# Attention, spectra, convolution, merge and experts in one block of a diffusion-transformer layer, with the first filter set computed in attention's tail

## The reference

```python
hx = _rms(x, norm1) * (1 + sc1) + sh1
zx = hx @ w_in
y_a = _hyena(zx[..., :OFF_Q], conv_w, conv_b, _hyena_filters(L, *filt), hyena_bias)
q, k, v = ...                                   # 8 heads, 2 key/value heads, rotary
y_b = _window_attention(q, k, v, kc, vc, attn_sink)
x_new = x + g1 * _merge(y_a, y_b, zx[..., OFF_G:], w_branch_a, w_branch_b, w_out)
hx2 = _rms(x_new, norm2) * (1 + sc2) + sh2
x_new = x_new + g2 * _expert_choice(hx2, router, w_gate, w_up, w_down)

# in _hyena_filters: four sets (2 orders x 2 halves of the channels) in the kernel
h = (h @ fout).reshape(L, HYENA_ORDER, 2, HYENA_W) * decay
k = jnp.concatenate([h[:, :, 0], zeros, h[:0:-1, :, 1]], axis=0)
return jnp.fft.rfft(k, axis=0)                  # the spectra

# in _expert_choice
aff = jax.nn.softmax(h @ router, axis=-1)
g, idx = lax.top_k(jnp.swapaxes(aff, 1, 2), cap)    # cap = 128 tokens for each expert
```

## Time and profile before

| | us |
|---|---|
| median of 3 runs (lowest, highest) | 2165.69 (2163.97, 2168.26) |
| the profiled execution, its own time | 2169.22 |
| span of its trace | 2167.4 |
| busy in the span: PE, DVE, ACT, POOL | 2125.7, 1683.4, 1174.8, 192.9 |
| DMA moved, mean rate | 540.62 MB, 249 GB/s |

### The profile page before, as it was taken

One profiled execution on the slowest core, in us unless ns is written; L12 is line 12 of the kernel. 1 busy time (PEld: TensorE's weight loads), 2 busy tenths in 40 slices (PEclk: granted clock), 3 DMA queues, 4 the chain that ended last, 5 costly groups with the idle time before them and its releaser, 6 DMA issues.

```text
span 2167.4 us, 28107 instructions
## 1 busy us (share of the span) xinstructions
PE 2125.7 (98%) x10395; PEld 1705.1 (79%) x10395; DVE 1683.4 (78%) x1820; ACT 1174.8 (54%) x1274; POOL 192.9 (9%) x85
## 2 busy tenths in 40 slices
PE   9999999989989999999999999999999999999998
PEld 4988888766669777788678888888888888888886
DVE  4667765258775999854889889898898998989986
ACT  4421222156521222334267777777777787777775
POOL 1000000000000000300001111010110111011100
PEclk9999999999999999999899999999999999999999
DMA  8234354130012234543599999999999999999993
GB/s 316 66 104 159 132 189 151 47 127 15 16 49 78 78 117 183 164 163 117 216 409 401 401 400 380 402 382 378 379 386 400 382 378 378 390 398 378 380 377 112
DMA packets 183003, 540.62 MB, mean 249 GB/s; under 512 B 14597, under 2 KB 56935, under 8 KB 182288
## 3 DMA queue, kind: packets, MB, share of 16 engines
q1 hardware_dynamic: 172872, 507.85, 62.1%
q0 software_dynamic: 5264, 17.00, 3.0%
q10 hardware_dynamic: 4792, 14.74, 1.7%
HBM read 503.90 MB, written 35.65 MB: 249 GB/s over the span
## 4 chain that ended last, share of the span: by engine, by line
PE 51%; POOL 0%; issue 0%; DVE 0%; POOLq 0%
PE p_y L312 5%; PE p_y L314 5%; PE p_y L313 5%; PE p_b L312 5%; PE p_b L314 5%; PE p_b L313 5%; PE p_a L314 5%; PE p_a L312 5%; PE p_a L313 5%; PE p_t L2875 1%; PE p_a L2905 1%; PE p_t L2866 1%; PE p_b L2905 1%; PE p_y L2961 0%; POOL out_x L2678 0%
## 5 line engine op out<-in xcount | busy, mean ns | idle before, releaser
L2745 DVE TENSOR_TENSOR r_lo<-ring,r_hi 128x2048 fp32r<-128x2048 f32 x372 | 838.8, 2286 | 59.3 <-ACT r_hi L2706 58.1
L2706 ACT ACTIVATE r_hi<-ring 128x2048 fp32r<-128x2048 f32 x372 | 708.5, 1916 | 148.9 <-PE p_b L314 76.7
L312 PE MATMUL p_y<-r_hi,a_hi 128*128 128x512 f32 x512 | 205.3, 401 | 0.0
L314 PE MATMUL p_y<-r_hi,a_lo 128*128 128x512 f32 x512 | 199.9, 391 | 0.0
L313 PE MATMUL p_y<-r_lo,a_hi 128*128 128x512 f32 x512 | 199.2, 389 | 0.0
L312 PE MATMUL p_b<-r_hi,x_hi 128*128 128x512 f32 x496 | 193.1, 389 | 0.0
L314 PE MATMUL p_b<-r_hi,x_lo 128*128 128x512 f32 x496 | 193.0, 389 | 0.0
L313 PE MATMUL p_b<-r_lo,x_hi 128*128 128x512 f32 x496 | 192.9, 389 | 0.0
L312 PE MATMUL p_a<-r_hi,x_hi 128*128 128x512 f32 x480 | 189.8, 395 | 0.0
L314 PE MATMUL p_a<-r_hi,x_lo 128*128 128x512 f32 x480 | 187.3, 390 | 0.0
L313 PE MATMUL p_a<-r_lo,x_hi 128*128 128x512 f32 x480 | 186.8, 389 | 0.0
(11 more groups left out here) (415 smaller groups left out, 3915.0 us busy)
## 6 DMA issues: line engine op xcount, KB each, us to landing
ring<-in_w_gate SPq DMA_DIRECT2D x128, 1024.0 KB, 8.9
ring<-in_w_up SPq DMA_DIRECT2D x128, 1024.0 KB, 8.9
ring<-in_w_down SPq DMA_DIRECT2D x128, 1024.0 KB, 12.4
w_raw<-in_w_in SPq DMA_DIRECT2D x17, 1024.0 KB, 6.2
ada_rest<-in_ada_w SPq DMA_DIRECT2D x16, 1024.0 KB, 5.4
ada<-in_ada_w SPq DMA_DIRECT2D x8, 1024.0 KB, 15.1
gate_dram<-zs ACTq DMA_DIRECT2D x16, 512.0 KB, 2.6
x_normed<-gate_dram SPq DMA_DIRECT2D x16, 512.0 KB, 4.2
```

The lines of the kernel that those rows point to most:

```text
L312: pe.matmul(out, a_hi, b_hi, start=start, stop=False)
L314: return pe.matmul(out, a_lo, b_hi, start=False, stop=stop)
L2706: act.activation(r_hi[:, i % PARTS], ring[:, i % RAW], ACT.Copy).then_inc(hi_ready, 1)
L2745: dve.tensor_tensor(r_lo[:, i % PARTS], ring[:, i % RAW], r_hi[:, i % PARTS].bitcast(F32), ALU.subtract).then_inc(lo_ready, 1)
```

## The change

What it does:

- Attention, spectra, convolve, merge and experts stand in one block. Their functions are written first and called one behind the other on each engine. The two meetings of all engines between attention and spectra, and between merge and experts, are gone. `give_back` moves from behind attention to behind front.
- Attention's tail is taken out of attention and written into spectra: its steps alternate with the filters of set 0 on PE, DVE and ACT. The set has buffers of its own, `pm_first` and `pm_first_lo`, where the token matrices of front lay.
- The jobs of spectra get a new order and pairs of banks from a list: filters 0, one job of spectrum 0, two jobs of filters 1, one of spectrum 0, two of filters 1, two of spectrum 0, then as before. Two matrix instructions that filled behind attention go.
- SP loads the first biases once the last scores are made, ahead of the last two stores of attention; `ya` is loaded after spectrum 0.
- In merge the counts for tiles 1 to 4 come before the second half of tile 7's projection, a fill of 3 stands where the other counts stood, those come later, and the last fill is 3 in place of 6. The router's shift moves ahead of tile 1's second projection.
- In experts `turn_f` is signalled for every two chunks, the fills go from 4 to 1 and from 6 to 3, and single waits (`idx_ready`, `aff_copied`, `first_gated`, `x_stored`) take the place of the meeting.

The diff without its changes of indentation, cut:

```diff
+                g["g_stored"] = [nc.alloc_semaphore(name=f"g_stored{i}") for i in range(2)]
                 front(g)
+                give_back()
...
-                attention(g)
-            give_back()
+                zeroth = attention(g)
...
+                g["pm_first"] = sbw("pm_first", [P, NT, 2, HC])
...
+                g["pm_first_lo"] = sbw("pm_first_lo", [P, NT, 2, HC], F32R)
...
+            chosen = experts(g)
             with nc.Block() as block:
                 @block.sync
                 def _(sp):
...
+                    attention_sync(sp)
+                    spectra_sync_first(sp)
+                    attention_sync_last(sp)
                     spectra_sync(sp)
                     convolve_sync(sp)
                     merge_sync(sp)
+                    chosen[0](sp)
...
                 @block.tensor
                 def _(pe):
...
+                    zeroth[1](pe)
                     spectra_tensor(pe)
                     convolve_tensor(pe)
                     merge_tensor_first(pe)
                     convolve_tensor_last(pe)
                     merge_tensor(pe)
+                    chosen[1](pe)
...
+        f_jobs = [[("f", i, q) for q in Q] for i in range(SETS)]
+        s_jobs = [[("s", i, c, odd) for c in range(FC) for odd in range(2)] for i in range(SETS)]
+        later = f_jobs[2] + s_jobs[1] + f_jobs[3] + s_jobs[2] + s_jobs[3]
+        jobs = f_jobs[0] + s_jobs[0][:1] + f_jobs[1][:2] + s_jobs[0][1:2] + f_jobs[1][2:] + s_jobs[0][2:] + later
+        frees = f_jobs[0] + f_jobs[1][:1] + s_jobs[0][:1] + f_jobs[1][1:2] + s_jobs[0][1:2] + f_jobs[1][2:] + s_jobs[0][2:] + later
+        pairs = [0, 1, 0, 1, 2, 0, 1, 3, 0, 1, 2, 3] + [n % 4 for n in range(len(later))]
...
-            sp.dma_start(ya[:], g["z_dram"][0:HY, :].rearrange("(c p) t -> p c t", p=P)).then_inc(v_in, 16)
...
+        def spectra_sync_first(sp):
+            sp.wait_ge(s_done, U)
+            load_bias(sp, 0)
+            load_bias(sp, 1)
...
-            filters(0)
-            filters(1)
-            for i in range(SETS):
-                spectrum(i)
+            pe.wait_ge(fpm_ready, 2)
+            pe.wait_ge(exp_ready, U)
+            filters(0, range(0, 1))
+            for part in range(2):
+                values(pe, NT - 1, part)
+            turn_r(pe, NT - 1)
+            spread(pe, NT - 2)
+            for part in range(2, 5):
+                values(pe, NT - 1, part)
+            filters(0, range(1, 2))
+            pe.wait_ge(yb_ready, NT - 1)
+            spread(pe, NT - 1)
+            pe.wait_ge(table_low, TABLES)
+            pe.wait_ge(r_copied, NT)
+            pe.wait_ge(o_copied, NT)
+            spectrum(0, 0, 0)
+            filters(1, range(0, 1))
+            pe.wait_ge(c_copied, U)
+            pe.wait_ge(yb_ready, NT)
+            spectrum(0, 0, 1)
+            filters(1, range(1, 2))
+            spectrum(0, 1, 0)
+            spectrum(0, 1, 1)
+            filters(2)
...
+            denominators(dve, NT - 1)
+            whole(0, 0)
+            turned_copy(dve, NT - 1)
+            whole(0, 1)
+            divide(dve, NT - 2)
+            low_part(0, 0)
+            low_part(0, 1)
+            whole(0, 2)
+            whole(0, 3)
+            divide(dve, NT - 1)
...
-        jobs += [("p", 7), ("h", 6), ("l", 5), ("b", 4), ("q", 7), ("l", 6), ("b", 5), ("o", 7), ("h", 7), ("b", 6), ("c", 5),
+        jobs += [("p", 7), ("h", 6), ("l", 5), ("b", 4), ("q", 7), ("l", 6), ("b", 5), ("c", 4), ("o", 7), ("h", 7), ("b", 6), ("f", 3),
...
+            count_below(NT - 3)
             count_below(NT - 2)
-            pe.wait_ge(lg_ready, NT - 1)
-            fill(6)
+            fill(3)
...
+                    if k % 2:
                     ins.then_inc(turn_f, 1)
...
                 pe.wait_ge(raw_in[0], 16)
+            pe.wait_ge(g["aff_copied"], 1)
                 fill(2, 512)
-                fill(4, P)
+            fill(1, P)
                 for q in range(2):
                     turn_x(0, q, q, q)
-                fill(6, P)
+            fill(3, P)
+            pe.wait_ge(g["first_gated"], 1)
```

More of the change, by code:

```diff
@@ new lines, in values @@
+        def values(pe, n, part):
+            b = blocks(n)
+            tiles = [(i, t) for i, t in enumerate(b)] + [(3, NT), (4, NT + 1)]
+            if part >= len(tiles):
+                return
+            if part == 0:
+                pe.wait_ge(w_copied, NH * (n + 1))
+                pe.wait_ge(c_copied, NH * (n + 1))
+                if 0 < n < NT - 1:
+                    pe.wait_ge(yb_ready, n)
+            i, t = tiles[part]
+            for kv in range(NKV):
+                v = HD * (NG + kv)
+                mm = pe.matmul(values_bank(n)[HD * kv:HD * kv + HD, :], qkv[:, t, v:v + HD],
+                               pT[n % 2][kv][:, i].rearrange("p j t -> p (j t)"),
+                               start=part == 0, stop=part == len(tiles) - 1)
+            if part == len(tiles) - 1:
+                mm.then_inc(pv_done, 1)
@@ L1699, in spectra_vector, with even @@
-            filters(0)
-            filters(1)
-            for i in range(SETS):
-                spectrum(i)
+                for n in range(4):
+                    whole(i, n)
+                    if n:
+                        low_part(i, n - 1)
+                low_part(i, 3)
+            def even(i, c):
+                k, j = FC * i + c, ("s", i, c, 0)
+                if k >= 2:
+                    dve.wait_ge(ks_ready, k - 1)
+                dve.wait_ge(cp_ready, k + 1)
+                other = pj[:, pair[j], 1].rearrange("p (z n) -> p z n", z=2)
+                dve.tensor_tensor(half[:, k % 2, 0], cp[:, k % 2], other, ALU.add).then_inc(half_ready, 1)
+                dve.tensor_tensor(half[:, k % 2, 1], cp[:, k % 2], other, ALU.subtract).then_inc(freed, 1)
@@ new lines, in spectra_vector @@
+            denominators(dve, NT - 1)
[8 more added lines that the diff above has]
+            divide(dve, NT - 1)
+            low_part(0, 2)
+            low_part(0, 3)
+            whole(1, 0)
+            even(0, 0)
+            whole(1, 1)
+            low_part(1, 0)
+            low_part(1, 1)
+            both(0, 0)
@@ L1703, in spectra_vector @@
+            whole(1, 2)
+            whole(1, 3)
+            low_part(1, 2)
+            low_part(1, 3)
+            even(0, 1)
+            both(0, 1)
+            filters(2)
+            for i in range(1, SETS):
+                for c in range(FC):
+                    even(i, c)
+                    both(i, c)
                 if i + 2 < SETS:
@@ L2247, in merge_tensor @@
                         mm = count_below(n)
+                elif kind == "f":
+                    pe.wait_ge(lg_ready, NT - 1)
+                    mm = fill(t)
                 elif kind in "hi":
@@ new lines, in experts_sync, with body @@
+        def experts_sync(sp):
+            def body(e, first, last):
+                for i in range(EU):
+                    if first and i < EARLY_UNITS:
+                        continue
+                    if first and i == EARLY_UNITS:
+                        sp.wait_ge(gathered, 16)
+                    if first and i >= RAW:
+                        sp.wait_ge(unit_done, i - RAW + 1)
+                    if not first:
+                        sp.wait_ge(lo_ready, EU * e + i - RAW + 1 - NATIVE)
+                    load_unit(sp, g, e, i)
+            each_expert(sp, body)
```

1291 lines of the change are left out of this document (635 added, 656 removed).

## The result

The changed kernel takes 2150.91 us (median of 4 runs, 2150.49 to 2152.27), the kernel before beside it 2165.61: a ratio of 0.9931, with a 95% interval from 0.9919 to 0.9944, or 14.7 us less. The forecast was 2149.7, 16.0 less.

The account below looks back on a forecast made before the run. PE was taken as the bound, busy 2125.7 of 2167.4 us, with gains only in seams between stages. Terms -14.1 + 2.0 - 3.9 = -16.0 us took the median 2165.69 to 2149.7, range 2145.5 to 2156.0.

Parts of the forecast that it names:

- Attention's tail and spectra: Seam from attention to spectra: interleaving tail and filters without the meeting gains 14.1 us, bounds 11.7 to 15.2.
- my own prices: Attention's tail and spectra: assumed PE times, such as half a filter set 1.77 us, each half of `values` 1.75.
- the 0.3 us that PE was to wait for DVE: Spectrum 0: PE finishes half of filters 1 at 605.5, its odd job starts at 605.8 after DVE's low parts.
- The first rival: Attention's tail and spectra: DVE becomes the bound, hand-overs pile up; gain there 9 to 11.7, time 2152.1 to 2154.7; chance 0.18.
- Front seam: Front to attention: moving `give_back` here costs 2.0 us, between 1.5 and 3.2; PE's gap grows from 1.49 to 3.0.
- the 1.5 us for the meeting and the clearing: Front to attention: extra PE gap from `give_back`, taken as the difference between seams of 1.97 and 0.50 us.
- The 0.5 for the clock: Front to attention: 0.5 us allowed for low clock behind the longer gap, which could cost up to 1.7.
- Merge to experts: Seam from merge to experts: no meeting, shorter fills and two modulations fewer gain 3.9 us, bounds 3.0 to 5.0.
- ends in time, except by 0.5 at low clock: Merge to experts: PE's fill, 1.8 us at full or 3.6 at low clock, begins at about 1051, late by at most 0.5.
- The third rival: Seams at spectra, front and experts: no low clock at all; gain 18.7 us, time 2147.0; chance 0.08.
- The second rival: Low clock at attention's start (1.7) and expert 0's first products (up to 3.4); gain 11.6, time 2154.1; chance 0.12.
- The gain isn't passed on: Convolve or merge waits for something keeping its old time, leaving 3.9 less 2.0; time 2163.8; chance 0.03.

Follow-up runs that it names:

- e4_tail_apart: Changed kernel with attention's tail and the filters no longer interleaved, old order of jobs and bank pairs, still one block without the meeting; 2160.77 us, ratio 0.997.
- before: The kernel without the change; 2165.61 us beside the changed kernel's first runs.
- e1_before_again: The kernel without the change, run and traced once more, unchanged; 2168.29 us (11 runs).
- e2_shift_early: The kernel without the change, with only the router's shift moved ahead of tile 1's second projection; 2165.02 us, ratio 0.9993.
- e9_after_again: The changed kernel run and traced once more, unchanged; 2151.11 us (5 runs), ratio 0.9923.
- e7_short_fill: Changed kernel with PE's fill ahead of expert 0's tokens cut from two 128x512 products to one; 2152.62 us, ratio 0.9931.
- e11_both_fills: Changed kernel plus three unread 128x512 products in convolve and nine unread 128x128 products at front's end; 2151.04 us, ratio 0.9924.
- after: The changed kernel itself, with the whole change; 2150.91 us (median of 4 runs), ratio 0.9931.

## Why the prediction was right, step by step

**Attention's tail and spectra: 14.1 forecast, 13.0 measured.** The mechanism held: the turns of PE and DVE fit, no wait but the last one of 0.63, and e4_tail_apart shows that the order carries most of it. The term was mis-sized by my own prices. I took half a filter set at 1.77 us and two halves of `values` at 1.75 each, less than their length by an overlap of 0.2. In the trace the next one starts 1.92 behind a filter half and 1.87 behind a half of `values`. Four of the one and two of the other make 0.84 (the fifth filter half isn't on the path, since what follows it waits for DVE). I also rounded spectrum's instructions down to 0.12 each, where the 17.47 us for 144 that I took them from give 0.121; the three pieces of spectrum 0 took 17.85 in place of 17.28, 0.57 more. Against this, the 0.3 us that PE was to wait for DVE ahead of the first odd job did not come. And 1.25 of the 13.0 are the half clock behind the meeting, which the traces of before and e1_before_again have and that of e2_shift_early has not.

**The first rival** (DVE becomes the bound, 9 to 11.7) did not come: DVE was busy 30.16 of 34.20 us, and late nowhere in between.

**Front seam: 2.0 forecast, 0.95 in the first trace, up to 2.6 in the others.** The step that failed is the 1.5 us for the meeting and the clearing, taken from the difference of two seams (0.50 behind ACT's issue at the front, 1.97 behind SP's at attention's end). Measured it is 0.95, in which a meeting is 0.32 if both meetings cost the same. What the other half us at attention's end was, no run shows. The 0.5 for the clock was too little for an execution that has the fall (1.7) and too much for one that hasn't; seven traces of nine have it. (Rows 7 do not show the 3 to 4 us of low clock that I took from them; the seven traces have 3.4.) So the seam costs 0.95 or about 2.65, on either side of the 2.0, and the two errors offset each other only in part.

**Merge to experts: 3.9 forecast, 3.5 measured**, and it goes link by link in the first trace. Affinities to numbers: 5.67 to 4.77 us, 0.9 gained where I had 0.5. Numbers to gather: 3.47 to 1.15, 2.3 gained where I had 2.7; POOL starts 1.15 behind the numbers, not 0.8. Gather to transposes: 4.46 to 5.09, 0.6 lost. There I wrote that PE's fill "ends in time, except by 0.5 at low clock": it did begin at 1035.18 at half clock and ended 0.7 behind the landing. That is a draw too: from the gather to the transposes the traces with this seam have 4.22 to 5.18 us. Transposes to first product: 2.56 to 1.67, 0.9 gained where I had 1.0. The clock was full in expert 0's first products, as forecast, and the stage behind kept its length to 0.24.

**What was missed.** I had the router's shift in the list of what moves, and gave it no price. Its own length is the same in both places and cancels; what it stood next to was not looked at. Moving it gives 3.3 us where the fall comes. So the 14.7 us of the medians hold a gain that the forecast hadn't, beside a front seam that in most traces costs more than the first one shows and a spectra term that was too large. That the sum came within 1.3 us owes something to luck.

**Median and profile.** I carried the difference from the profiled execution over to the median. The means differ by 14.7 us in the first set of runs and by 16.6 in the set of e9_after_again (2150.99 against 2167.62), on both sides of the 16.0. But the profiled execution before lay at the upper end of a spread of over 6 us, and a sum made from it could have been 3 us off. The third rival (no low clock at these seams, gain 18.7) has the number of the traces' difference by chance: the clock was at half from about 1028 to 1039, over merge's end.

**The second rival** (low clock at dearer places) came by half: at attention's start in seven traces of nine, in expert 0's first products only in e7_short_fill. (Its 16.7 is 0.2 more than the terms give: 14.1 - 1.5 + 3.9 is 16.5.) **"The gain isn't passed on"** did not come, and e11_both_fills shows why it had to be asked of each stage: a gain of PE alone inside convolve is lost, while one that moves DVE's work as well is kept.

## What to carry to other kernels

Where two engines take turns across a stage's end, look for work of the next stage that needs only what has long been ready, and put it in the turns: this was worth twice as much here (8.6 us) as the meeting of the engines with its fill and the half clock behind it (4.3). Price each piece by the distance from its start to the next start, not by its length less a guess. And before a faster step is counted, look at which engine is full in the stage that follows.

## What the runs showed of the hardware

- The granted clock falls at a few places, and at some of them in one execution and not in another of the same kernel. Behind a gap of 2.45 us or more at attention's start it fell in seven traces of nine (1.7 us lost), behind one of 1.25 to 1.56 in none of five. It fell at the router (3.3 us lost), in convolve (nearly nothing lost, since DVE hides it) and at merge's end. Times of one kernel spread over 2.4 us (after, nine runs) and 8 us (before, over all sets), and the longer ones have the lower mean clock. So a difference of two single traces has one such draw of each in it.
- With 32 narrow matrix instructions (16 columns each) in a row and no idle time of PE, the clock went to half during the second 16 in all three traces that have them. With 16 at that place it stayed full in all eleven traces. "TensorE: Matmul & The Clock Gate", Part 1, of the Trainium skill says that the default is the throttled state and that activity releases it. From that sentence alone one would not expect this fall: the clock went to half here while the sums show PE busy for 2.00 of 2.00 us (before, 961 to 963).
- A cut in a fill that PE runs at half clock did not bring the work behind it forward in the one trace of it: the tokens were waited for, the clock came back later, and the first product was 0.6 us later than in after's first trace.
- A second meeting of all engines right behind a first one took 0.32 us on PE; a meeting with the clearing of the semaphores took 0.95.
